# Result rows of the last blocks moved, first loads regrouped, last stage in groups of two

## What is computed

```
h = x + 1/2 * postnorm(SwiGLU_1(prenorm(x)))            # FFN 1, hidden width 2816
n = prenorm(h);  [b | c | hh | u | v] = n @ W_in        # five parts of 512
    y_a = b * causal_conv3(c * hh)
    y_b = u * (tril(W_s[head]) @ rmsnorm(v) + b_s)      # chunks of 128 positions
h = h + postnorm(concat(rmsnorm(y_a), rmsnorm(y_b)) @ W_out)
h = h + 1/2 * postnorm(SwiGLU_2(prenorm(h)))            # FFN 2
h = h + norm(sigmoid(h @ W_pg) * (p @ W_pp))            # the last stage ("ple")
```

## Time and profile before

| | us |
|---|---|
| median of 3 runs | 1333.33 (1333.08 to 1335.34) |
| the profiled execution, its own time | 1332.94 |
| its span on the slowest core (core 2) | 1331.8 |
| spans of the 8 cores | 1326.5 to 1331.8 |
| PE busy, of the span | 1290.0 (97%) |
| DVE, ACT, POOL busy | 524.1, 411.3, 94.7 |
| mean granted clock of PE, over the cores | 0.989 to 0.993 |

### The profile page before, as it was taken

One profiled execution on the slowest core, in us unless ns is written; L12 is line 12 of the kernel. 1 busy time (PEld: TensorE's weight loads), 2 busy tenths in 40 slices (PEclk: granted clock), 3 DMA queues, 4 the chain that ended last, 5 costly groups with the idle time before them and its releaser, 6 DMA issues.

```text
span 1331.8 us, 18723 instructions; the slowest of 8 cores (1326.5 to 1331.8 us)
## 1 busy us (share of the span) xinstructions
PE 1290.0 (97%) x6734; PEld 651.8 (49%) x6816; DVE 524.1 (39%) x694; ACT 411.3 (31%) x862; POOL 94.7 (7%) x185
## 2 busy tenths in 40 slices
PE   8999999999999999999998999999999999999995
PEld 6566664455545666654443344444444444444442
DVE  3222222447696222213266321223477922122237
ACT  3311112344465111111166211123334721111136
POOL 2110000001001100000001100000010011000000
PEclk9999999999999999999999899999999999999998
DMA  8999322129725963231289994332297299333123
GB/s 186 201 208 207 65 48 48 24 39 178 123 49 108 168 110 64 48 72 25 48 176 257 215 182 79 58 62 32 48 179 130 56 144 175 69 63 58 32 40 126
DMA packets 88906, 139.89 MB, mean 105 GB/s; under 512 B 58352, under 2 KB 58608, under 8 KB 88432
## 3 DMA queue, kind: packets, MB, share of 16 engines
q0 software_dynamic: 25296, 90.25, 41.1%
q1 hardware_dynamic: 63520, 48.43, 13.5%
HBM read 206.03 MB, written 9.51 MB: 162 GB/s over the span
## 4 chain that ended last, share of the span: by engine, by line
PE 85%; DVE 5%; ACT 4%; DMA 3%; issue 3%; SPq 0%; ACTq 0%; DVEq 0%
PE ps L212 56%; PE ps L557 24%; PE ps L546 3%; DVE nT L221 1%; DMA y<-big 1%; DMA nT<-nbr 1%; ACT big L217 1%; DMA h<-xT 1%; DVE big L225 1%; DVE big L221 1%; ACT sg L217 1%; DVE nbr L221 1%; ACT L217 1%; PE ps L711 1%; ACT nbr L217 1%
## 5 line engine op out<-in xcount | busy, mean ns | idle before, releaser
L212 PE MATMUL ps<-nT,ring 128*128 128x384 bf16 (+1 forms) x4127 | 776.6, 349 | 16.4 <-DVE nT L221 7.9
L212 PEld LDWEIGHTS ps<-nT,ring 128*128 128x128 bf16 x4160 | 407.9, 98 | 381.4 <-issue 29.4
L225 DVE TENSOR_TENSOR big<-ps,sg 128x384 bf16<-128x384 f32 (+1 forms) x220 | 134.0, 611 | 489.3 <-PE ps L212 469.8
L557 PE MATMUL ps<-ring,big 128*128 128x512 bf16 x1291 | 283.7, 379 | 1.5
L217 ACT ACTIVATE sg<-ps 128x384 f32<-128x384 f32 (+1 forms) x237 | 127.0, 537 | 500.9 <-PE ps L212 490.3
L557 PEld LDWEIGHTS ps<-ring,big 128*128 128x128 bf16 x1320 | 129.2, 98 | 155.5
L253 POOL DMA_DIRECT2D ring<-w x170 | 90.2, 539 | 1066.7 <-PE ps L212 461.5
L217 ACT ACTIVATE big<-ps 128x1024 bf16<-128x1024 f32 (+4 forms) x89 | 75.4, 862 | 226.3 <-PE ps L557 195.2
L225 DVE TENSOR_TENSOR zsc<-ps,gains 128x1024 f32<-128x1024 f32 x51 | 62.3, 1222 | 180.2 <-ACT big L217 180.1
L557 PE MATMUL ps<-ring,nT 128*128 128x512 bf16 x470 | 104.9, 379 | 2.1 <-DVE big L225 1.4
L557 PEld LDWEIGHTS ps<-ring,nT 128*128 128x128 bf16 x480 | 46.8, 98 | 58.3 <-issue 2.5
(11 more groups left out here) (73 smaller groups left out, 363.5 us busy)
## 6 DMA issues: line engine op xcount, KB each, us to landing
ring<-w POOLq DMA_DIRECT2D x170, 512.0 KB, 15.1
h<-x SPq DMA_DIRECT2D x17, 512.0 KB, 30.2
gains<-gain SPq DMA_DIRECT2D x12, 512.0 KB, 9.2
y<-big SPq DMA_DIRECT2D x12, 512.0 KB, 10.8
big<-xT SPq DMA_DIRECT2D x2, 2048.0 KB, 13.8
y<-zsc SPq DMA_DIRECT2D x4, 512.0 KB, 6.2
h<-xT SPq DMA_DIRECT2D x4, 384.0 KB, 5.9
h<-xT SPq DMA_DIRECT2D x2, 768.0 KB, 10.7
```

The lines of the kernel that those rows point to most:

```text
L212: ins = nc.tensor.matmul(out_ap, l, r, start=(i == 0), stop=(i == n - 1))
L225: return DVE.mark(nc.vector.tensor_tensor(out=out, in0=in0, in1=in1, op=op))
L557: ins = nc.tensor.matmul(o.t, lhs(k), sv, start=(k == 0), stop=(k == nk - 1))
```

## The change

Three places are edited. (1) `gb` gives blocks 6 and up the columns from 8192 on, `gb_guard` and `guard1` follow. (2) The first x tile comes in 2 DMAs, the second in 1, POOL starts the fills when the first tile has landed; three slots are heads in pass 0, and the third tile's normalisation is hooked one unit later; the norm of the last block ahead of FFN 2 goes behind the first unit of FFN 2, with the loads and fills that followed it. (3) Pass 1's last stage has groups [0,1], [2,3], [4,5], [6,7]; the third goes through a new `middle_two`, with two small activations that load a table.

```
     def gb(b):
-        i = b % 6
-        return zsc_t[:, i - 4, :] if i >= 4 else bigf[:, 1024 * i:1024 * (i + 1)]
+        if b in (4, 5):
+            return zsc_t[:, b - 4, :]
+        o = 1024 * b if b < 4 else 8192 + 1024 * (b - 6)
+        return bigf[:, o:o + 1024]
...
-    xt_load(PASSES[0], 0, 4)
+    xt_load(PASSES[0], 0, 2)
     ev_gc = gc_sem.add(nc.sync.dma_start(out=gc_t[:], in_=gcol_d))
-    xt_load(PASSES[0], 1, 2)
+    xt_load(PASSES[0], 1)
...
-    POOL.wait(xt_ev[0, 1][0])
+    POOL.wait(xt_ev[0, 0][3])
...
-        if pend is not None:
-            pre_fn(*pend)
-        return e
+        return pend
...
+        def zg_of(b):
+            return bigf[:, 4096 + 1024 * (b - 4):4096 + 1024 * (b - 3)]
+        def table(func):
+            nxt["tab"] = act([nxt.get("tab")], out=sv_t[:, 0, 0, 0:1], in_=ones_t[:, 0:1], func=func)
+        def middle_two(b0, b1):
+            for b in (b0, b1):
+                sigmoid(b, gate(b, False))
+            table(AF.Ln)
+            st = {}
+            for b in (b0, b1):
+                product(b, *embed(b, False))
+            for b in (b0, b1):
+                st[b] = rstd_of(gb(b), sg_t[:].rearrange("p a s -> p (a s)"), [zev[b]], D)
+                st[b] += (tt([zev[b], gain_ev[base + GPLE]], zg_of(b), gb(b), gain(base + GPLE), ALU.mult),)
+            table(AF.Sigmoid)
+            for b in (b0, b1):
+                r, e3, e1, ez = st[b]
+                out_ev[b] = store(b, stt([e3, e1, ez], gb(b), zg_of(b), r, h_t[:, b, :], ALU.mult, ALU.add))
...
+            if N is None and gi == len(groups) - 2:
+                middle_two(*grp)
+                continue
...
     def gb_guard(b):
-        return [guards["zsc"] if b % 6 >= 4 else None, out_ev.get(b - 6) if b >= 6 else None]
+        if b in (4, 5):
+            return [guards["zsc"]]
+        return [xn_ev[1, 0][-1]] if b >= 6 and (1, 0) in xn_ev else []
...
-            evs = [out_ev.get(x + 6 if x < 3 else x) for x in range(lo, hi + 1) if x < 4]
-            if hi >= 4:
-                evs += [xn_ev[1, 1][-1], xn_ev[1, 0][-1]]
+            evs = []
+            for x in range(lo, hi + 1):
+                if x < 4:
+                    evs.append(out_ev[x])
+                elif x < 8:
+                    evs.append(xn_ev[1, 1][-1])
+                else:
+                    evs += [xn_ev[1, 0][-1], out_ev[x - 2] if x < 11 else None]
...
-            gu_stage(P, 2, guard1, {(1, 0): (1, start_square), (1, 1): (0, start_mid), (2, 0): (0, start_loads),
+            gu_stage(P, 3, guard1, {(1, 1): (1, start_square), (2, 0): (1, start_mid), (3, 0): (0, start_loads),
                                     (8, 0): (0, late_consts)},
-                     [(0, 0), (0, 1), (1, 0), (1, 1), (0, 2), (1, 2)])
+                     [(0, 0), (0, 1), (1, 0), (1, 1), (2, 0), (2, 1), (0, 2), (1, 2), (2, 2)])
...
+        def last_norm(P=P):
+            pre_ffn2(*pend)
+            gain_load(base + GPLE, [last_pre["ev"]])
+            gain_load(base + NGAIN + G1POST, [last_pre["ev"]])
+            POOL.wait(vo_last, last_pre["ev"])
...
+            pay_owed([nT_ev[P.nb - 1]])
+        gu_stage(P, 3, guard_none, {(0, 0): (1, last_norm)})
...
-        groups = [[0, 1, 2], [3, 4, 5], [6, 7, 8]] if P.nb == 9 else [[0, 1, 2], [3, 4, 5], [6, 7]]
+        groups = [[0, 1, 2], [3, 4, 5], [6, 7, 8]] if P.nb == 9 else [[0, 1], [2, 3], [4, 5], [6, 7]]
```

More of the change, by code:

```diff
@@ L894, in finish @@
                 h_free[b] = e
+        def zg_of(b):
[16 more added lines that the diff above has]
+                out_ev[b] = store(b, stt([e3, e1, ez], gb(b), zg_of(b), r, h_t[:, b, :], ALU.mult, ALU.add))
         def last_two(b0, b1):
-            zg = [bigf[:, 4096:4096 + D], bigf[:, 4096 + D:4096 + 2 * D]]
-            junk = bigf[:, 4096 + 2 * D:4096 + 3 * D]
+            zg = [zg_of(b0), zg_of(b1)]
+            junk = bigf[:, 10240:10240 + D]
             gp = gain(base + GPLE)
@@ L1052, in build_program @@
         nT_ev.clear()
[L1053 to L1065, removed]
+        pre_ffn2 = pre_mid(base + G2PRE)
+        pend = tok_stage(P, 8, 2, lambda b, k: nT_t[:, k, b * 128:(b + 1) * 128], lambda b: [norm_ev[b]],
+                         base + GMPOST, 1.0, 3, 0, pre_ffn2, {0: tail})
+        ple_in = {}
+        def last_norm(P=P):
[3 more added lines that the diff above has]
+            POOL.wait(vo_last, last_pre["ev"])
+            for i, r0 in enumerate(sorted(set([P.rows[0]] + ([P.rows[8]] if P.nb == 9 else [])))):
+                n = 1024 if i == 0 else 128
+                ple_in["ev"] = pt_sem.add(nc.gpsimd.dma_start(out=pT_v[:, :, i * 1024:i * 1024 + n],
+                                                              in_=pT_d[:, :, r0:r0 + n]))
+            pay_owed([nT_ev[P.nb - 1]])
+        gu_stage(P, 3, guard_none, {(0, 0): (1, last_norm)})
+        pT_ev = ple_in["ev"]
         hold_fills(1)
```

## The result

| | before | after |
|---|---|---|
| median, us | 1333.89 (1333.08 to 1335.34, 4 runs) | 1313.16 (1312.09 to 1314.16, 4 runs) |
| ratio | | 0.9843, 95% 0.9826 to 0.9860 |
| profiled execution, its own time | 1332.94 | 1312.09 |
| span, slowest core | 1331.8 (core 2) | 1311.0 (core 4) |
| spans of the 8 cores | 1326.5 to 1331.8 | 1307.8 to 1311.0 |

The forecast was 1313.7, within 1309.5 to 1319.5.

The account below looks back on a forecast made before the run. PE was taken as the bound, busy 1290.0 of 1331.8 us. Terms -11.0 - 3.7 - 0.5 - 2.0 - 2.2 = -19.4 took 1332.94 to 1313.5 (1313.9 for the median); forecast 1313.7, range 1309.5 to 1319.5.

Parts of the forecast that it names:

- Start of pass 1, -11.0: Start of pass 1: DVE no longer waits for late stores, PE runs through; 11.0 us less, bounds 9 and 11.6.
- The rival that the wait would only change its name: Start of pass 1: stores of blocks 0 to 3 are as late, the 11.0 stays, 1324.7 us; chance 0.03.
- The margin of 0.2 us: Start of pass 1: `x_apply` ends at 733.0, its last step is needed at 733.2, so no stall.
- the rival with 0.12: Start of pass 1: `x_apply` late, PE idles over 3 us, clock falls, some 5 us kept, 1318.7; chance 0.12.
- Third x tile, -3.7: Third x tile, pass 0: a whole unit behind x_stat cuts the 4.4 us break to a 0.7 rest; 3.7 us less.
- Norm ahead of FFN 2, -2.0: FFN 2, pass 0 alone: first Silu no longer behind the last block's norm, bank free earlier; 2.0 us less.
- Last stage, -2.2: Pass 1's last stage: block 6's product starts 2.2 us earlier, the chain behind it unchanged; bounds 0 and 3.5.
- The laid-out order: Last stage: instruction lists laid out with traced start-to-start costs; old order gives 1318.95 for product 6, new order 1316.7.
- Start, -0.5: Kernel start: earlier fills, but a later second x tile and 1.2 GHz again; 0.5 us less, bounds -2.7 and +1.5.
- L: Kernel start: landing time of the second x tile, 15.2 without sharing, taken as 16.5; PE ready at L + 4.8.
- The half-share bound of 17.5: Kernel start: fills take half of every engine from 11.4 on, so the second x tile lands near 17.5.
- the rival's +1.5: Kernel start: turns between queues delay the x tile, +1.5 us in place of -0.5, total 1315.7; chance 0.15.

Follow-up runs that it names:

- e2: Kernel before with only the changed first loads (first x tile in 2 DMAs, second in 1, fills from the first tile's landing): 1331.41 us, ratio 0.9979.
- e3: Kernel before with only three head units and the third x tile's normalisation one unit later: 1331.23 us, ratio 0.9980.
- e4: Kernel before with only the last block's norm moved behind the first unit of FFN 2: 1331.65 us, ratio 0.9978.
- e1: Kernel before with only the new rooms of blocks 6 to 8 and their guards: 1323.10 us, ratio 0.9914.
- e5: Kernel before with only pass 1's last stage changed (groups of two, `middle_two`, tables loaded early): 1333.32 us, ratio 0.9987.
- e11: Full change with the second x tile's normalisation in pass 1 hooked half a unit (one bank) later: 1317.11 us, ratio 0.9868.
- e10: Full change with the third x tile's squares and normalisation hooked half a unit earlier: 1311.95 us, ratio 0.9828.
- e6: Full change with `middle_two` taken out, groups of two all in the general way: 1316.18 us, ratio 0.9862.
- e7: Full change without the two small activations that load a table early: 1315.01 us, ratio 0.9853.
- the filler: Full change plus 8 unused matmuls in the mixer's first wait of pass 0: 1312.80 us, ratio 0.9833.

## Why the prediction came out right

The total was 19.4 less by forecast and 20.8 by the profiled executions. The five single parts add up to 21.6, so they neither help nor hinder one another within the intervals.

The profiles allow a finer test, since every core runs the same list. Means over the 8 cores, in us; "single" is the kernel with that part alone. The start is the first unit's, reckoned at full clock (start of the 64th up matmul less 63 x 0.162); the stages run from their first matmul to the next stage's first or to the end.

| stretch | before | after | less | single | forecast |
|---|---|---|---|---|---|
| start | 21.9 | 20.2 | 1.7 | 20.5 (e2) | 0.5 |
| FFN 1 up, pass 0, behind it | 177.4 | 173.7 | 3.6 | 173.8 (e3) | 3.7 |
| FFN 2 up, pass 0 | 173.6 | 171.7 | 2.0 | 171.7 (e4) | 2.0 |
| FFN 1 up, pass 1 | 165.1 | 153.7 | 11.4 | 153.7 (e1) | 11.0 |
| last stage, pass 1 | 49.4 | 47.3 | 2.1 | 47.2 (e5) | 2.2 |

Together 20.9, the whole difference of the mean spans (1330.0 and 1309.2). Each part moves its own stretch, and the other four of a single-part kernel stay within 1.0 us of before. Term by term, with the slowest cores in detail:

**Start of pass 1, -11.0: right.** From x_stat's first matmul behind the two units to the first gate of the last stage is a stretch that both traces have: 723.03 to 1282.42 before (559.4), 715.74 to 1263.85 after (548.1), 11.3 less. e1 gives 11.5. The rival that the wait would only change its name fell: DVE has no wait for `y<-big` in that stretch, its waits from 690 to 750 after are
```profile
DVE big L227 <- PE ps L214: 17.8, 7, 2.8
...
DVE nT L223 <- ACT ps L219: 2.7, 1, 2.7
```
The margin of 0.2 us that I gave `x_apply` was real: it started 4.62 behind x_stat (4.65 forecast), and e11, which puts the same work one bank (3.45 us) later, lost 3.4 us in the cores that kept the clock. So the rival with 0.12 was the right one to fear, and lay one hook away.

**Third x tile, -3.7: right.** A rest of 0.8 us was left (forecast 0.7): the 40th matmul from 48.04 on would start at 54.37 undisturbed and starts at 55.16. That makes 3.6. e3 alone gave 2.7 [1.3, 4.0], e10 removed the rest. That the gaps would be too small to cost the clock was right: with two heads 26 of 40 cores fell there (before, e1, e2, e4, e5), with three heads none of 72.

**Norm ahead of FFN 2, -2.0: right.** The up stage is 2.0 us shorter in every core, of the changed kernel and of e4 alike. e4's median gave 2.9 [1.6, 4.3]; the interval holds 2.0. Between the slowest cores the way from FFN 2's first matmul to pass 1 took 302.4 us (406.79 to 709.22) and 300.7 (401.19 to 701.93), 1.7 less: 0.3 us came back behind the up stage. In pass 1 PE's wait stayed (1.2 before, 1.1 after).

**Last stage, -2.2: right.** 1282.42 to the end of the span was 49.4 us, 1263.85 to the end is 47.15: 2.2 less. The laid-out order gave 34.3 us to product 6, and 34.37 was measured; e6 and e7 split it into the order (1.1) and the early tables (1.2). The table load to the next activation stayed at 1.29 to 1.30 us (1295.70 to 1297.00), with 31 loads in the kernel instead of 25. The rule of "ScalarE: Activation LUTs" in the Trainium skill ("What ACT_TABLE_LOAD costs") that a drain of 1.38 us stands on top was the alternative, with a term near 0. No trace here shows the drain: a load and the rule's drain would put 2.7 us where 1.3 stand, and a load follows within 0.1 us of the end of the activation ahead of it when that is all it waits for.

**Start, -0.5: the step that was mis-sized; measured -3.1 between the two slowest cores, -1.7 on average over the eight (e2's median 2.8).** The failed step is "I expect 1.2 GHz again, one us more for the warm-up and 1.2 us on the first unit". The granted clock was 1.00 over 20 to 26 us in all 8 cores after, and the first unit came 4.4 us behind the squares' start on core 4 (forecast 4.8, and 2.2 for the clock on top). In full-clock terms the start stands at 20.74 instead of 23.88, 0.4 beyond my bound of -2.7. The thin stretch before it (two matmuls every 0.73 us) can cost the clock, but it is the rarer case: in the 7 kernels that load this tile in one piece 12 of 56 cores fell to 1.2 GHz between 17 and 24 us. The first unit, at full clock, stands 4.5 us behind the tile's landing in each of the 44 others and 5.4 to 6.1 in these 12. So the cost was 0.9 to 1.7 us with a chance of about 0.2, and I had put 2.2 us in as certain. I took the stretch ahead of the fall at 50 for the same case; the outcome there was the fall in 26 of 40 cores. There PE waits step by step for `x_apply`; here it has two matmuls in every square and one pause of up to 2.2 us. Which of the two features decides was not tried.

Part of the gain is in what before paid: its slowest core and two others fell at the start, the other five did not (19 of 40 cores over the five kernels with the old loads). On the three the start came 1.8 to 4.0 us earlier, on the five 0.3 to 1.8.

That L came out so near (squares at 16.34, forecast 16.5) is luck, since my reason for it does not hold. The fills' first packets move only 1.9 to 3.1 us after POOL's issue (core 4: at 13.6, issued at 10.46), when all but 0.2 to 0.3 MB of the tile's 1.5 have passed; from 13 to 15 us both queues are busy (52.8 and 39.3% of the engines' time). So the fills share only with the tile's last part. Over the eight cores it landed at 14.7 to 16.4, on average 15.7, and before, with hardly a packet of a fill beside it, at 15.2 to 15.9, on average 15.5; over all kernels with the new and the old loads the averages are 16.0 (56 cores) and 15.5 (40 cores). The half-share bound of 17.5 by the Trainium skill's turns between queues ("DMA: Bandwidth & Descriptors", "Queues, rings and completion order") supposes that the turns begin at 11.4; they did not, and the runs say nothing against the turns themselves. Its working has a slip too: 11.4 + 4.4 is 15.8, not 17.5, and the rival's +1.5 needs an L of 18.5. What I read in the earlier trace rows as a slow rise of the fills' share (0.25 over 14 to 16) is the same delay between issue and first packet, and a mean of 0.61 there means three quarters of the stretch at 1.2 GHz, not half.

**Not foreseen: the mixer, +1.7 on core 4.** The mixer's waits are the same in all cores (1.03 and 0.55 us near 322), yet core 4 alone fell to 1.2 GHz for 16 matmuls. Core 4 of the kernel before, not its slowest, shows the same fall at 329; the other kernels of the study show it in 0 to 3 cores. Nothing ties it to the change, and it decided which core was slowest. So the 11.3 + 3.1 + 3.6 + 1.7 + 2.2 = 21.9 us gained in the five places came to 20.8 in span. That remainder, 1.1, is the 1.7 less small differences elsewhere (0.3 us in the mixer's waits).

So for the slowest cores the forecast's closeness owes something to two errors that nearly cancel: 2.6 us too little at the start, 1.7 us unforeseen in the mixer. In the means over the cores, where the mixer drops out (one core fell before and one after), what is left is 1.2 us too little at the start and 0.4 at the start of pass 1.

## What to carry to other kernels

A room is free when its store has landed, not when it was issued: here the stores around the start of pass 1 landed 10 to 15 us after issue on the slowest core, block 6's after 10.5. Give the next stage's first results the rooms whose stores are oldest, and look for the engine queued behind that wait; here DVE's three waits, 13.5 us together, cost 11 us of PE.

A short idle is worth more than its length where the granted clock falls behind it, so put the price of both into the sum, but as two cases with a chance each: behind the mixer's waits (1.03 and 0.55 us) it fell in some cores of the same program and not in others. And read the waits on more than the slowest core: at the start of the kernel before, three cores fell and five did not.

Splitting a group is worth what it takes off the chain: `middle_two` with its early tables gained 2.3 us, the smaller groups by themselves nothing.

## What the runs showed of the chip

The lower clock is not the same in all cores of one program, even where the list and the waits are the same. At the start of the kernel before, core 4 ran its first 16 matmuls at full clock behind 2.20 us of idle, core 0 fell behind 2.23 and the slowest core behind 3.71. At the start of pass 1 core 5 had its 16 matmuls in 3.61 us behind 2.42 us of idle, and core 2 ran them slowly behind 2.91. It is not the length of the idle alone: in the mixer far shorter waits (1.03 and 0.55 us, equal in all cores of the changed kernel) were followed by the fall in 0 to 3 of 8 cores, 14 of 96 in all without the filler.

Where the waits went, the fall went too. At the start of pass 1 all 40 cores of the five kernels with the old rooms fell, and none of the 64 cores of the eight kernels with the new rooms and the hook in its place; with the hook one bank late, 6 of 8.

Fills issued by POOL beside a load of x on SP had their first packet 1.9 to 3.1 us after issue in the changed kernel. The tile landed on average 0.5 us later than with the old loads (16.0 over 56 cores against 15.5 over 40).
